# First latent head's parts and twelve gate products ahead of a synchronisation, and projections over four bank pairs

## The reference

```python
q = (rms_norm(c_q, q_norm_g) @ w_uq).reshape(B, T, 8, 96)          # 8 heads of the latent attention
q_nope, q_pe = q[..., :64], apply_rope(q[..., 64:], cos_m, sin_m)
kv = (rms_norm(c_kv, kv_norm_g) @ w_ukv).reshape(B, T, 8, 128)
k_nope, v_m = kv[..., :64], kv[..., 64:]
o_m = mla_attention(q_nope, q_pe, k_nope, k_pe, v_m)               # causal softmax attention
o_n = nsa_attention(...)                                           # the other attention, done before
y = sigmoid(gate_m) * (o_m @ w_proj_mla) + sigmoid(gate_n) * (o_n @ w_proj_nsa)
return y @ w_out                                                   # gate_m, gate_n = x @ w_in[...]
```

## Time and profile before

| | |
|---|---|
| median of three runs | 3033.03 us |
| profiled execution | 3040.43 us, its span 3038.6 us |
| mean granted clock of TensorE | 0.97 of 2.4 GHz |
| busy: TensorE | 2933.9 us (97%) |
| busy: VectorE, ScalarE, GpSimd | 1513.7 (50%), 1213.2 (40%), 1163.8 us (38%) |
| chain that ended last | TensorE 82%, VectorE 9%, ScalarE 3%, DMA 2%, issue 2% |
| transfers | 324.15 MB, 107 GB/s in the mean |

### The profile page before, as it was taken

One profiled execution on the slowest core, in us unless ns is written; L12 is line 12 of the kernel. 1 busy time (PEld: TensorE's weight loads), 2 busy tenths in 40 slices (PEclk: granted clock), 3 DMA queues, 4 the chain that ended last, 5 costly groups with the idle time before them and its releaser, 6 DMA issues.

```text
span 3038.6 us, 37806 instructions
## 1 busy us (share of the span) xinstructions
PE 2933.9 (97%) x13559; PEld 2352.8 (77%) x13559; DVE 1513.7 (50%) x2649; ACT 1213.2 (40%) x1851; POOL 1163.8 (38%) x598
## 2 busy tenths in 40 slices
PE   9999999998999999999999999899999998998997
PEld 7888888767788888888888867778888876775665
DVE  4441365555644414443155555664431887447665
ACT  4332133765353322433232476443331352425553
POOL 4444353512354443544443451244444332112221
PEclk9999999999999999999999999999999998799998
DMA  4333232102323331323332311323332121016995
GB/s 150 95 98 113 86 116 91 53 25 91 111 90 97 102 105 64 101 96 102 105 104 93 98 32 35 124 71 108 97 110 95 50 89 49 28 63 239 343 357 196
DMA packets 118574, 324.15 MB, mean 107 GB/s; under 512 B 12464, under 2 KB 48688, under 8 KB 117936
## 3 DMA queue, kind: packets, MB, share of 16 engines
q1 hardware_dynamic: 109024, 305.17, 30.8%
q10 hardware_dynamic: 2800, 8.91, 0.8%
q0 software_dynamic: 6624, 8.41, 0.8%
HBM read 313.52 MB, written 24.64 MB: 111 GB/s over the span
## 4 chain that ended last, share of the span: by engine, by line
PE 82%; DVE 9%; ACT 3%; DMA 2%; issue 2%; POOL 1%; DVEq 0%; SPq 0%; another core or an unknown queue 0%; ACTq 0%; POOLq 0%
PE ps L429 18%; PE ps L430 18%; PE ps L432 18%; PE ps L464 4%; PE ps L2134 2%; PE ps L1035 2%; PE ps L929 1%; DVE cacc L2437 1%; PE ps L2120 1%; PE ps L1019 1%; PE ps L2122 1%; PE ps L2121 1%; DMA mraw<-in_w 1%; PE ps L572 1%; PE ps L1893 1%
## 5 line engine op out<-in xcount | busy, mean ns | idle before, releaser
L2873 POOL TENSOR_TENSOR wlo<-raw,whi 128x1024 fp32r<-128x1024 f32 (+1 forms) x368 | 955.0, 2596 | 1446.8 <-ACT whi L627 1446.4
L627 ACT ACTIVATE whi<-raw 128x1024 fp32r<-128x1024 f32 (+1 forms) x368 | 409.1, 1112 | 720.6 <-PE ps L432 608.4
L429 PE MATMUL ps<-xlo,whi 128*128 128x512 f32 x1704 | 666.0, 391 | 2.2 <-POOL wlo L2873 1.6
L430 PE MATMUL ps<-xhi,wlo 128*128 128x512 f32 x1704 | 663.8, 390 | 0.0
L432 PE MATMUL ps<-xhi,whi 128*128 128x512 f32 x1704 | 420.8, 389 | 0.0
L429 PEld LDWEIGHTS ps<-xlo,whi 128*128 128x128 f32 x1704 | 320.5, 188 | 70.1 <-POOL wlo L2873 2.0
L430 PEld LDWEIGHTS ps<-xhi,wlo 128*128 128x128 f32 x1704 | 320.4, 188 | 66.0
L432 PEld LDWEIGHTS ps<-xhi,whi 128*128 128x128 f32 x1704 | 319.8, 188 | 66.4
L429 PE MATMUL ps<-hlo,whi 128*128 128x512 f32 x704 | 277.3, 394 | 0.0
L430 PE MATMUL ps<-hhi,wlo 128*128 128x512 f32 x704 | 275.5, 391 | 0.0
L759 DVE SCALAR_TENSOR_TENSOR xa<-ps,xa 128x512 f32<-128x512 f32 x48 | 33.1, 689 | 360.9 <-PE ps L432 350.4
(11 more groups left out here) (623 smaller groups left out, 4897.3 us busy)
## 6 DMA issues: line engine op xcount, KB each, us to landing
raw<-in_gu SPq DMA_DIRECT2D x176, 512.0 KB, 3.5
raw<-in_mix SPq DMA_DIRECT2D x96, 512.0 KB, 3.6
mraw<-in_w SPq DMA_DIRECT2D x23, 2048.0 KB, 12.4
raw<-in_dn SPq DMA_DIRECT2D x64, 704.0 KB, 4.0
mdraw<-in_w SPq DMA_DIRECT2D x23, 1024.0 KB, 13.2
raw<-in_w SPq DMA_DIRECT2D x32, 512.0 KB, 3.5
gate_rows<-tails SPq DMA_DIRECT2D x32, 256.0 KB, 4.3
sgmn<-gate_rows SPq DMA_DIRECT2D x16, 512.0 KB, 3.9
```

What stands on the lines that cost most here:

```text
L429: nc.tensor.matmul(out, whi[:, slot, cols], rlo, start=first and t == 0, stop=False)
L430: nc.tensor.matmul(out, wlo[:, slot, cols], rhi, start=False, stop=False)
L627: nc.scalar.activation(whi[:, s, 0:n], raw[:, r, 0:n], ACT.Copy).then_inc(hi_done, 1)
L2873: nc.gpsimd.tensor_tensor(wlo[:, s, 0:n], raw[:, r, 0:n], whi[:, s, 0:n].bitcast(F32), ALU.subtract).then_inc(w_ready, 1)
```

## The change

Three things are done, in both layers.

First, the parts of head 0 are made in the first stage: ScalarE's four conversions behind its work of tile 9, VectorE's three subtractions behind tile 10. They go to `mla_odd`, since `mla_even` lies where the inputs of the 14 tiles still are; the heads change places. In the second stage VectorE counts up their semaphores with no work.

Second, TensorE's filler in that synchronisation is replaced by the first 12 matmuls of gate 12. So each later gate is whole four units earlier (behind units 3, 11, 19 and 27), and the last four units have no gate products. Since gate 12 uses bank 0 now ahead of the synchronisation, the 14 tiles take their banks in another order, 0 and 1 last, the wait for the gate copies moves from tiles 0 and 1 to tiles 4 and 5, and TensorE waits for VectorE's move of tile 10 ahead of the gate.

Third, the projections use four bank pairs, (0, 6), (1, 7), (2, 4), (3, 5). Projections 0 to 3 wait for no tile; from 4 on, projection m waits for the two products of VectorE that read the banks of m - 4. The output pair waits for the readers of its own bank and, matmul by matmul, for the tile that it takes next.

```diff
-    NSA_GATES, NSA_FEED, MLA_FEED = 7, 4, 3
+    NSA_GATES, NSA_FEED, MLA_FEED, MLA_LEAD = 7, 4, 3, 12
+    def pe_mla_gates(pe, L, first, count):
+        n_gate, k = divmod(first, 3 * KT)
+        if N_EARLY + n_gate < N_GATES:
+            pe_gate(pe, L, N_EARLY + n_gate, k, k + count)
     def mla_gate(u):
-        n, at_end = divmod((u + 1) * MLA_FEED, 3 * KT)
+        n, at_end = divmod((u + 1) * MLA_FEED + MLA_LEAD, 3 * KT)
-            x = mla_parts[h % 2]
+            x = mla_parts[(h + 1) % 2]
-    MLA_BANK = (0, 1, 4, 5, 2, 3)
+    MLA_BANK = (2, 3, 4, 5, 0, 1)
@@ pe_mixer, the 14 tiles
-            if n < 2:
-                pe.wait_ge(gate_raw, L * N_GATES + (N_EARLY - 1 + n))
+            if n in (4, 5):
+                pe.wait_ge(gate_raw, L * N_GATES + (N_EARLY - 1 + n - 4))
-            if n < 2:
-                pe.wait_ge(S["tile_free"], t + 1)
-            elif n >= 6 and n % 2 == 0:
+            if n >= 6 and n % 2 == 0:
                 pe.wait_ge(S["tile_free"], T_UQ + 2 + n // 2 - 2)
+        pe.wait_ge(S["tile_free"], T_UQ + 2 + 6)
@@ pe_mixer_out
         def feed(u):
-            n_gate, k = divmod(u * MLA_FEED, 3 * KT)
-            if N_EARLY + n_gate < N_GATES:
-                pe_gate(pe, L, N_EARLY + n_gate, k, k + MLA_FEED)
+            pe_mla_gates(pe, L, MLA_LEAD + u * MLA_FEED, MLA_FEED)
-        pe.wait_ge(S["mix_used"], 2)
         for m in range(KT):
-            pe.wait_ge(S["mix_used"], m + 1)
+            if m >= 4:
+                pe.wait_ge(S["y_own"], 4 * (m - 4) + 2)
@@ pe_out_pair
-            if j == 0:
-                pe.wait_ge(S["mix_used"], 2 + KT - 1)
-            else:
-                pe.wait_ge(S["y_own"], 4 * (KT - 1) + 2)
+            pe.wait_ge(S["y_own"], 4 * (4 + j) + 2)
             for k in range(KT - 1):
+                if j == 0:
+                    pe.wait_ge(S["mix_used"], 2 + k + 1)
                 add(j, k)
     def proj_bank(m, s_):
-        return ps[(m % 2) if s_ else 6 + m % 2][:]
+        return ps[m % 4 if s_ else (6, 7, 4, 5)[m % 4]][:]
@@ act_mixer, behind tile 9
+            if n == 9:
+                (q_hi, q), (k_hi, k) = mla_part(0, 0, 0), mla_part(0, 1, 0)
+                act.wait_ge(S["rotated"], 2)
+                act.wait_ge(S["tile_moved"], 4)
+                nc.scalar.activation(q[64:96], q_rot[0:32, 0, :], ACT.Copy).then_inc(S["qkhi_ready"], 1)
+                nc.scalar.activation(k_hi[64:96], k_pe[64:96, :], ACT.Copy)
+                act.wait_ge(S["tile_free"], T_UQ + 2 + 1)
+                nc.scalar.activation(k_hi[0:64], k[0:64], ACT.Copy).then_inc(S["qkhi_ready"], 1)
+                act.wait_ge(S["qkhi_ready"], 5)
+                nc.scalar.activation(q_hi, q, ACT.Copy).then_inc(S["qkhi_ready"], 1)
@@ act_mixer_out
-        for x in range(2):
-            head_hi(0, x)
@@ dve_mixer, behind tile 10
+            if n == 10:
+                (q_hi, q), (k_hi, k) = mla_part(0, 0, 0), mla_part(0, 1, 0)
+                (q_lo, _), (k_lo, _) = mla_part(0, 0, 1), mla_part(0, 1, 1)
+                dve.wait_ge(S["qkhi_ready"], 7)
+                own.link(nc.vector.tensor_tensor(q_lo, q, q_hi.bitcast(F32), ALU.subtract))
+                own.link(nc.vector.tensor_tensor(k_lo[64:96], k_pe[64:96, :], k_hi[64:96].bitcast(F32), ALU.subtract))
+                own.link(nc.vector.tensor_tensor(k_lo[0:64], k[0:64], k_hi[0:64].bitcast(F32), ALU.subtract))
@@ dve_mixer_out
-        for x in range(2):
-            head_lo(0, x)
+        dve.sem_inc(S["qkhi_ready"], 2)
+        dve.sem_inc(S["qklo_ready"], 2)
@@ TensorE's program
-            sync_point(pe, "pe", lambda: pe_idle(8, ps[7]))
+            sync_point(pe, "pe", lambda: pe_mla_gates(pe, L, 0, MLA_LEAD))
```

More of the change, by code:

```diff
@@ L1320, in proj_bank @@
     def proj_bank(m, s_):
-        return ps[(m % 2) if s_ else 6 + m % 2][:]
+        return ps[m % 4 if s_ else (6, 7, 4, 5)[m % 4]][:]
     def mla_part(h, x, part):
-        return mla_parts[h % 2][0:96, 2 * x + part, :], (q_mla, k_mla)[x][0:96, h, :]
+        return mla_parts[(h + 1) % 2][0:96, 2 * x + part, :], (q_mla, k_mla)[x][0:96, h, :]
     def act_mixer(act, L):
@@ L1403, in head_hi @@
                                      ).then_inc(S["kpe_copied"], 1)
-                act.wait_ge(S["kpe_copied"], h + 1)
+                act.wait_ge(S["kpe_copied"], h)
                 nc.scalar.activation(to, of, ACT.Copy).then_inc(S["qkhi_ready"], 1)
```

## The result

| | us |
|---|---|
| before, 13 runs | 3023.78 (3016.64 to 3040.73) |
| after, 13 runs | 2999.08 (2993.64 to 3013.74) |
| ratio after/before | 0.9919 (95%: 0.9903 to 0.9936) |
| forecast | 3014.2 (3004 to 3025), from a base of 3033.03: ratio 0.9938 |

The kernel became 24.5 us faster by the ratio (19.4 to 29.3), 24.7 between the medians; the forecast was 18.8. The sign, the mechanisms and the places were right; two sizes were not, the base and the price of one projection.

What follows compares the result with a forecast made beforehand. TensorE was taken as the limit almost everywhere, so its removed waits count in full. Per layer 7.4 + 1.5 + 0.5 = 9.4 us, two layers 18.8, from the median 3033.03 to 3014.2 us; range 3004 to 3025.

Steps and rivals of the forecast that it cites:

- the base: Whole kernel: median of the three runs shown, 3033.03 us, from which the forecast gain was taken.
- the price of one projection: Projections on TensorE: one takes 28.20 / 5 = 5.64 us at full clock, six 33.84.
- Part 1: Projections over four bank pairs: TensorE's wait for ylo and the slow clock behind it go, 7.4 us a layer.
- the bound of 7.7: Projections: upper bound of the gain a layer, with 0.15 us of idle and small waits gone as well.
- The room of 2.6 us: Output pair: tile 7 ends at 780.8, needed at 783.4; waits one by one make this room.
- Part 2: Head 0's parts ahead of the synchronisation: first score earlier, VectorE last to synchronise, 1.5 us a layer.
- Part 3: Last head: 12 gate products made earlier save 2.1 us, a meeting of splits costs 1.8; +0.5 us a layer.
- The lower bound of this part: Last head: -2.0 us a layer, as with less filler the clock may go down sooner.
- Rival A: Output pair: the stall moves there, TensorE waits for tile 7 with slow clock behind; 3026.6 us, chance 0.12.
- Rival B: Last head: TensorE has less to do in units 28 to 31, the clock falls; 3021.0 us, chance 0.20.
- Rival C: VectorE's tiles in the projections: two splits in each make the kernel slower, 3045 us, chance 0.04.
- the range: Whole kernel: 3004 to 3025 us, bounds without the worst corner and some 4 us below for run spread.

Runs made afterwards that it cites:

- part 1 alone: The kernel before with four bank pairs, waits for the reads only and the output pair's waits one by one; 3012.61 us, ratio 0.9969.
- ten fillers: The kernel before with ten filler matmuls on TensorE in front of projection 2; 3025.78 us, ratio 1.0011.
- filled ends: The changed kernel with filler matmuls in TensorE's waits of the first and last units and behind the 12 gate products; 3002.3 us, ratio 0.9918.
- part 3 alone: The kernel before with 12 gate products in the synchronisation in place of filler, head 0's parts still behind it; 3026.0 us, ratio 1.0009.
- four pairs, whole: The changed kernel with projection m waiting for the whole tile m - 4, not only the reads of its banks; 2998.88 us, ratio 0.9946.
- the two filler runs: The kernel before with 10 or 15 filler matmuls on TensorE in front of projection 2; 3025.78 us (1.0011) and 3015.39 us (0.9969).
- all three edits: The changed kernel with filler, o_nsa splits kept out of unit 29, and the last gate's store ahead of block 37's load; 2991.91 us, ratio 0.9889.

## Why the prediction came out as it did

**Part 1, 7.4 forecast, 8.5 measured (D of part 1 alone).** The mechanism, the place and the clock were right: no wait at projection 2, a clock of 1.00, and the slow clock behind the wait caused by it. The step of the sum that failed is "One takes 28.20 / 5 = 5.64 us at full clock". Without a wait one takes 32.96 / 6 = 5.49. The 28.20 us weren't all work: three more of the waits that the change lifts stood at their edges, for ylo at projections 4 and 6 and at the output pair. The weight loads of the kernel before show the first two, each behind ylo of the tile two before:

```profile
757.42 0.69 DVE L1700 TENSOR_TENSOR ylo<-sgmn,yhi 128x512 f32 x1
758.17 0.19 PEld L429 LDWEIGHTS ps<-otlo,whi 128*128 128x128 f32 x1 [0.52 <-DVE ylo L1700]
...
769.52 0.19 PEld L429 LDWEIGHTS ps<-otlo,whi 128*128 128x128 f32 x1 [0.48 <-DVE ylo L1700]
```

and at the pair the first product (780.95) stands behind ylo of tile 6 (whole at 780.80). The earlier trace rows doesn't show them as idle (28.05 of 28.20 busy), since the modelled ends of the matmuls reach over such gaps. By their starts the projections 3 to 7 took 5.74, 5.62, 5.73, 5.61 and 5.82 us (752.43 to 780.95), 1.05 more than five of 5.49. From start to start the 8.45 us of layer 0 are the wait of 5.1, the slow clock of 2.3 and this 1.05. It lies beyond the bound of 7.7, which added only the idle time shown. The pitch of the products would have told: 24 in a projection, 0.229 us apart, 5.49.

**The room of 2.6 us.** It was less. TensorE came to the pair sooner by the cheaper projections, VectorE took 31.95 us for tiles 2 to 7 (745.97 to 777.92), 5.33 a tile instead of 5.2, and the first to be late was tile 6 and not tile 7, since block 0 asks for it 18 products after its start. The forecast priced tile 7 alone; by its own numbers tile 6 had the smaller room, 2.2 us (whole at 775.6, asked for at 777.8). In the changed kernel that came to 0.7 us in one layer of two. The statement that the pair's waits make the room stands: with the old ones 6 to 7 us a layer are lost.

**Part 2, 1.5 forecast, 1.5 to 1.7 measured.** VectorE was the last to the synchronisation, the gate products were free. That nothing was to be taken for the clock was right: the first score is reached sooner, and in the changed kernel the slow clock stands in head 1.

**Part 3, +0.5 forecast, 0.2 as profiled, 1.1 at full clock.** The one long subtraction came (2.73 us) and was on the chain. Its price was 1.25 us and not 1.8, although it took 2.04 us more than alone; what covers the rest isn't shown. The products' own gain was larger than 2.1 less that, but the clock took it back. From the first score of head 6 to projection 0 the kernel before took 22.22 us where it ran at full level (ten fillers), 23.04 as profiled; with part 3 it was 21.09 at full level (filled ends), and 22.84 with part 3 alone. So 1.1 us is there, 2.4 from the products and the drain less 1.25, and a slow drain leaves 0.2, which is less than the 0.8 by which the kernel before differs with itself. In the changed kernel the stretch took 21.54 and 21.70, in four pairs, whole, 22.86 and 22.60, with the same instructions. The lower bound of this part had named the clock. The Trainium skill, SBUF — State Buffer, section "SBUF: two separate sides", lets a GpSimd instruction and a VectorE instruction with two SBUF inputs, whichever starts first, keep the shared ports for its whole length. By that the subtraction would end its own 0.69 us behind the split. The trace agrees to 0.14 us: it started behind the split and ended at 713.56, 0.55 us after it (713.01).

**Rivals.** Rival A came true where TensorE was made faster still, or the pair's old waits put back; in the changed kernel itself it was 0.7 us in one layer. Rival B, the clock in the last head: the first products of projection 0 (stretch C) take 2.85 to 5.27 us from one execution to the next, with and without the change, so a slow clock stands there, but it isn't shown as a consequence of the change. Rival C, two splits in every tile: only tile 0 had two.

**The base and the range.** By the traces the sum was 18.8 forecast and 21.1 measured (17.0 in D, 3.3 in A, 0.8 in B, C and E, where 14.8, 3.0 and 1.0 stood), by the runs 24.5 (19.4 to 29.3). Put on the median of 13 runs the forecast would have been 3005. The range took 4 us for the spread of the runs, where the three runs shown already spanned 15; their median was off by 9.3. So the base, 3033.03 where 13 runs have 3023.78, is the step behind the larger part of the miss. Why those three were slow isn't on record; the execution profiled with them, 3040.43 us, had a mean clock of 0.970.

## What to carry over

Price a wait between two instructions of its stage, by the pitch of the work and not by the idle time shown, add the slow clock that stands behind it, and give the base of the forecast the spread of its own runs. A wait that is lifted hands the bound to the next in line: here from about a third to all of what TensorE won ahead of the output pair was lost in the pair, until one store left its place in a queue. Waiting only for what is needed (the reads, tile by tile) did nearly as much as more buffers.

## What was not expected of the hardware

The same instructions in front of the same twelve products left TensorE at the lower level for none or for nearly all of them (2.85 to 5.01 us in the kernel before and the two filler runs), so one trace doesn't tell whether an edit caused a slow stretch. What decides it isn't shown; with filler in the waits (filled ends, all three edits) it was 2.84 or 2.85 in all four layers, without filler there at that level in 4 of 24.

VectorE's scaling yhi, with a single input, is held by GpSimd's split as the subtractions are: 2.05 us at 737.91 in the changed kernel, ending 0.28 us behind the two splits (734.45 + 5.23 = 739.68), and 0.43 us where no split runs.
